# Kernel on one core of Trainium2: the first recurrence chunk is prepared before the stage barrier, the GLA normalization moves up half a unit, and the chunk state is updated behind the next chunk's inverse

## What is computed

```python
h = _rmsnorm(x, norm1_g) * (1.0 + sc1) + sh1
proj = h @ w_in                                  # IN_PROJ = 3328 + 3088 + 2048 columns
x_rwkv = p_rwkv + (prev - p_rwkv) * rwkv_mu      # token shift of the RWKV part
y_r, s_rwkv_new = _rwkv7(x_rwkv, s_rwkv, ...)    # 16 heads of 64, matrix state per head
y_g, s_gla_new = _gla(p_gla, s_gla, ...)         # 4 heads, chunks of 64
...
# _rwkv7, per row t and head:
sa = einsum('bhij,bhj->bhi', S, -kk_t)
S = S * w_t + sa * (kk_t * a_t) + v_t * k_t
y = einsum('bhij,bhj->bhi', S, r_t)
# _gla ends with
o = o * lax.rsqrt(jnp.mean(o * o, axis=-1, keepdims=True) + EPS) * norm_g
out = o.reshape(B, T, GLA_DV_TOTAL) * jax.nn.silu(r)
```

## Time and profile before

| | |
|---|---|
| median of 3 runs | 1526.92 us (1526.65, 1526.92, 1533.84) |
| the profiled execution | 1532.53 us, its span 1530.8 us |
| PE busy | 1339.8 us (88%), 13407 matmuls |
| DVE, ACT, POOL busy | 595.9, 453.4, 240.9 us |
| first block's last matmul | starts 574.37 us |
| second block's first matmul | starts 586.00 us |
| second block's first product of power 2 | starts 593.27 us |
| first expert load issued | 985.66 us |

### The profile page before, as it was taken

The page is one execution under the profiler, slowest core; times in us unless marked ns, Lnnn a source line. Parts: engine busy times, 40 slices in busy tenths (PEclk is TensorE's granted clock), DMA queues, the critical chain, the costliest instruction groups (busy, mean ns, idle before and its releaser), DMA issues. The chain is left out here.

```text
span 1530.8 us, 30353 instructions
## 1 busy us (share of the span) xinstructions
PE 1339.8 (88%) x13407; PEld 988.8 (65%) x13407; DVE 595.9 (39%) x1041; ACT 453.4 (30%) x727; POOL 240.9 (16%) x250
## 2 busy tenths in 40 slices
PE   5999999999999995888779999879888878888784
PEld 1788999898998994777769997643333323333231
DVE  3322234442235445666455658523212121221117
ACT  2333244444555453343344533200000000000002
POOL 3000000000112113334211102001111111111105
PEclk9999999999999998999899999969999988999997
DMA  8566452233422210000312391299999999999984
GB/s 322 182 202 210 131 181 83 65 109 99 143 85 70 70 36 18 4 4 4 132 30 67 104 296 52 111 405 424 427 427 425 427 426 427 426 427 427 427 369 164
DMA packets 128634, 323.05 MB, mean 211 GB/s; under 512 B 13865, under 2 KB 99075, under 8 KB 112594
## 3 DMA queue, kind: packets, MB, share of 16 engines
q1 hardware_dynamic: 114304, 289.53, 49.5%
q10 hardware_dynamic: 7522, 15.57, 2.9%
q0 software_dynamic: 6672, 15.95, 2.9%
HBM read 303.51 MB, written 25.11 MB: 215 GB/s over the span
## 5 line engine op out<-in xcount | busy, mean ns | idle before, releaser
L806 PE MATMUL bank<-upper_r 128*128 128x272 f32 x3168 | 420.0, 292 | 5.4 <-DVE upper_r L1047 5.4
L806 PEld LDWEIGHTS bank<-upper_r 128*128 128x128 f32 x3168 | 404.2, 190 | 27.7 <-issue 26.4
L2677 PE MATMUL bank<-upper7b,lower 128*64 128x512 f32 x912 | 258.2, 663 | 69.7 <-issue 68.9
L2677 PEld LDWEIGHTS bank<-upper7b,lower 128*64 128x64 f32 x912 | 83.6, 152 | 207.5 <-issue 205.3
L1024 DVE TENSOR_TENSOR upper_r<-upper,upper_r 128x1024 fp32r<-128x1024 f32 x66 | 82.1, 1244 | 284.3 <-ACT upper_r L578 284.2
L2481 ACT ACTIVATE lower<-bank 128x256 f32<-128x256 f32 x32 | 12.3, 385 | 437.6 <-PE bank L2686 437.6
L3031 DVE COPY lower<-bank 128x512 f32<-128x512 f32 x32 | 22.1, 692 | 277.6 <-PE bank L2677 277.6
L2540 PE MATMUL bank<-upper_r 128*128 128x272 f32 x768 | 102.9, 294 | 3.2 <-DVE upper_r L2926 3.2
L2540 PEld LDWEIGHTS bank<-upper_r 128*128 128x128 f32 x768 | 99.3, 191 | 5.9 <-DVE upper_r L2758 3.6
L2699 PE MATMUL bank<-upper7b,lower 128*64 128x512 f32 x432 | 98.3, 596 | 0.0
L2286 POOL DMA_INDIRECT expert_out<-lower x30 | 44.5, 1484 | 220.6 <-DVE lower L3054 210.7
(11 more groups left out here) (410 smaller groups left out, 1809.1 us busy)
## 6 DMA issues: line engine op xcount, KB each, us to landing
upper7b<-in_expert_w_gate SPq DMA_DIRECT2D x29, 2048.0 KB, 30.9
upper7b<-in_expert_w_up SPq DMA_DIRECT2D x28, 2048.0 KB, 33.1
upper7b<-in_expert_w_down SPq DMA_DIRECT2D x27, 2048.0 KB, 27.6
upper<-in_w_in SPq DMA_DIRECT2D x66, 512.0 KB, 3.8
lower<-in_w_ada SPq DMA_DIRECT2D x23, 1024.0 KB, 5.0
lower<-in_expert_w_down SPq DMA_DIRECT2D x5, 2048.0 KB, 30.0
lower<-in_expert_w_up SPq DMA_DIRECT2D x4, 2048.0 KB, 36.5
lower<-in_expert_w_gate SPq DMA_DIRECT2D x3, 2048.0 KB, 30.9
```

The costliest lines, as they stand in the source:

```text
L806: m = mm(psum[s][:, c, 0:HALF], w_part[s][:, k, :], h_part[:, k, c * HALF:(c + 1) * HALF], start=k == 0 and w_part is w_high and h_part is ...
L2677: m = nc.tensor.matmul(psum[s][64 * b:64 * b + 64, 1, :], x_t[(e // 2) % 2][:, k, s * BLK:(s + 1) * BLK], w[:, k, :], start=k == 0, stop=k ...
```

## The change

Three things are moved. (1) In the GLA the squares go from j = 7 to 6, the mean and the root from 8 to 7, the transposes and the gate product from 10 to 9; `PREP_SLOT` goes from 84 to 82, so that the preparation ends in unit 64. (2) The entry of chunk 0 (two exponentials, alphas, queries, keys, an identity) goes from behind the barrier into the first block, next to unit 65; its six semaphores outlive the barrier, and the buffers are laid out anew: the rounded operands of the projection now stand at the end of the arena, the entry's results where the weight slots and the low-rank weights were. (3) `state(c)` goes behind `inverse(c+1)` in DVE's list, with a third buffer for `lam_end`. The layout of the regions is left out of the diff.

```diff
-        PREP_SLOT = 84
+        PREP_SLOT = 82
...
-                    if 0 <= slot - GLA_SLOT - 8 * i < 11]
+                    if 0 <= slot - GLA_SLOT - 8 * i < 10]
...
+        decays = sem("decays", lasting=True)
...
+                pool.wait_ge(w_mm, KD)
+                pool.wait_ge(a_mm, KD)
+                pool.tensor_copy(ari_first[:, :, P:192], id_w.unsqueeze(1).broadcast_to([P, 8, 64])).then_inc(fixed, 1)
+                pool.wait_ge(decays, 2)
+                pool.tensor_tensor(ari_first[:, :, 64:P], p_rw[:, 0:8, 0:64], lam_c, ALU.mult).then_inc(r_done, 1)
...
-                        if j == 7:
+                        if j == 6:
                             gla_squares(i, w, nc_)
-                        if j == 8:
+                        if j == 7:
                             gla_rows(i, w, nc_)
...
+                    if u == NU - 1:
+                        act.wait_ge(bon_mm, KD)
+                        for c in range(2):
+                            nc.scalar.activation(bon[c], psum[3][32 * c:32 * c + 16, c, 0:HALF], ACT.Copy
+                                                 ).then_inc(bon_done, 1)
+                        act.wait_ge(lam_done, 2 * KD)
+                        act.wait_ge(w_split, NU)
+                        nc.scalar.activation(lam_c, lam[:, :, 0:64], ACT.Exp).then_inc(decays, 1)
+                        nc.scalar.activation(lam_i, lam[:, :, 0:64], ACT.Exp, scale=-1.0).then_inc(decays, 1)
+                        nc.scalar.activation(c_sig, c_raw, ACT.Sigmoid).then_inc(c_sig_done, 1)
                     out(u, kind, f)
...
-                        if j == 10:
+                        if j == 9:
                             pe.wait_ge(o_done, 4 * i + 4)
...
-                    if phase == 0:
+                    if phase == (0 if k else 1):
                         if k == 0:
                             v.wait_ge(mixed, 10)
                             v.wait_ge(y_g_kept, 16 * 5)
...
+                v.wait_ge(kk_done, KD)
+                v.wait_ge(w_mm, KD)
+                v.wait_ge(a_mm, KD)
+                ve.tensor_scalar(ari_first[:, :, 0:1], kk[:, :, 0:1], -1.0, None, ALU.mult).then_inc(alpha_done, 1)
+                v.wait_ge(decays, 2)
+                ve.tensor_copy(lam_end_first, lam_c[:, :, 63]).then_inc(end_done, 1)
+                ve.scalar_tensor_tensor(out=ari_first[:, :, 1:64], in0=kk[:, :, 1:64], scalar=-1.0, in1=lam_c[:, :, 0:63],
+                                        op0=ALU.mult, op1=ALU.mult).then_inc(alpha_done, 1)
+                v.wait_ge(ka_done, KD)
+                v.wait_ge(w_split, NU)
+                for n, p in enumerate((slice(0, 64), slice(64, 128))):
+                    ve.tensor_tensor(bk_first[p, :, n, :], ka[p, :, 0:64], lam_i[p], ALU.mult).then_inc(bk_done, 1)
+                    ve.tensor_tensor(bk_first[p, :, 1 - n, :], p_rw[p, 8:16, 0:64], lam_i[p], ALU.mult).then_inc(bk_done, 1)
                 v.wait_ge(ends_tr, 1)
                 ve.tensor_copy(ends_t[0:52, :], bank(4)[0:52, 0:128]).then_inc(ends_t_done, 1)
...
-                identity(0)
                 pool.memset(t64, 0.0).then_inc(fixed, 1)
...
-                queries(0)
                 identity(1)
...
-                decay(0)
                 decay(1)
...
-                    if c >= 2:
-                        v.wait_ge(s_done, c - 1)
-                    nc.vector.tensor_copy(lam_end[c % 2], lam_c[:, :, CH - 1]).then_inc(end_done, 1)
+                    if c >= 3:
+                        v.wait_ge(s_done, c - 2)
+                    nc.vector.tensor_copy(lam_end[c % 3], lam_c[:, :, CH - 1]).then_inc(end_done, 1)
...
                         power(c + 1, 2)
-                    state(c)
-                    if more:
                         masked(c + 1, 2)
...
                         inverse(c + 1)
+                    state(c)
+                    if more:
                         inverse_off(c + 1)
```

More of the change, by code:

```diff
@@ L215, in build @@
         alpha_up = sq[:, 0:512]
+        first_at = chunk_at
+        W1 = Region(first_at)
+        bk_first = W1.take(8, 2, 64)
+        lam_c = W1.take(8, 64)
+        lam_i = W1.take(8, 64)
+        W2 = Region(z_at)
+        ari_first = W2.take(8, 192)
+        lam_end_first = W2.take(8)
         xa = rkr
@@ L1201, in _ @@
                 v.wait_ge(ends_t_done, 1)
-                v.wait_ge(kk_done, KD)
         clear_semaphores()
-        lay_out_upper(3, 0, MID)
+        live.extend((decays, alpha_done, r_done, bk_done, end_done, fixed))
+        lay_out_end("3", F32)
         NCK = NCH + 1
-        S4 = Region(chunk_at)
-        ari = [S4.take(8, 192) for _ in range(3)]
-        bk = [S4.take(8, 2, CH) for _ in range(2)]
+        S4 = Region(end_at)
         z4 = [S4.take(8, 2, P) for _ in range(2)]
@@ L1220, in build @@
         u0 = S4.take(8, CH)
-        s_h = [S4.take(8, CH) for _ in range(2)]
-        s_smp = S4.take(8, CH)
-        lam_c = S4.take(8, CH)
-        lam_i = S4.take(8, CH)
-        lam_end = [S4.take(8) for _ in range(2)]
+        bk_second = S4.take(8, 2, CH)
+        S5 = Region(first_at, z_at)
+        bk = [S5.take(8, 2, CH), bk_second]
+        lam_c = S5.take(8, CH)
+        lam_i = S5.take(8, CH)
+        s_second = S5.take(8, CH)
+        s_smp = S5.take(8, CH)
+        S6 = Region(z_at, end_at)
+        ari = [S6.take(8, 192)]
+        lam_end = [S6.take(8)]
+        ari += [S6.take(8, 192) for _ in range(2)]
+        lam_end += [S6.take(8) for _ in range(2)]
+        s_h = [S6.take(8, CH), s_second]
         st_rows_in = z4[1][0:64].rearrange("i j h n -> i (j h n)")[:, 0:D].rearrange("i (j n) -> i j n", n=P)
@@ L1552, in state_rows @@
                                               psum[s][0:64, b, :]).then_inc(st_rows, 1)
-                alphas(0)
-                for p, n in zip(HEADS, range(2)):
-                    nc.vector.tensor_tensor(bk[0][p, :, n, :], ka[p, :, 0:CH], lam_i[p], ALU.mult).then_inc(bk_done, 1)
-                    nc.vector.tensor_tensor(bk[0][p, :, 1 - n, :], p_rw[p, 8:16, 0:CH], lam_i[p], ALU.mult
-                                            ).then_inc(bk_done, 1)
-                for s in range(2):
-                    v.wait_ge(spilled[s], 16 * 8)
                 first_powers(0)
@@ L1570, in _ @@
                 alphas(1)
+                for s in range(2):
+                    v.wait_ge(spilled[s], 16 * 8)
                 v.wait_ge(st_in_tr, 1)
```

49 lines of the change are left out of this document (30 added, 19 removed).

## The result

The changed kernel takes 1513.85 us (median of 4 runs, 1511.33 to 1515.15) and the kernel before, beside it, 1529.18 us; the ratio is 0.9894, 95% interval 0.9863 to 0.9925: 15.3 us less between the medians. The profiled execution took 1514.58 us, its span 1512.7.

A forecast was written before the change was run, and what follows sets the result against it. The expert-weight stream bounds the tail, so TensorE's waits before its start at 985.6 us count: GLA 10.9, entry 5.0 and chunks 1.6 sum to 17.5 us, from 1526.92 to 1509.4 us; range for 8 in 10, 1504 to 1517.

The forecast's parts named there:

- The first rival: GLA tiles 0, 3 and 4: table loads and exits make a split late, 6.0 us back, 1515.4; chance 0.11.
- the room of 0.6: GLA tile 3: the split starts at 344.2, TensorE wants unit 37's weights at 344.8, so it just fits by 0.6 us.
- The fourth: Rival: GLA waits have another releaser and chunk savings go into stalls; only 5 us won, 1521.9; chance 0.06.
- the barrier took 1.8 us, and up to 0.8 more: Barrier exit: 1.8 us behind VectorE as last engine, up to 0.8 more for SyncE's transfers; taken as 579.4.
- at 588.3: Entry: power 2 starts at 588.3 instead of 593.27, behind POOL's sum, a gain of 5.0 us.
- the second rival: Entry's gain given back at POOL's sum and by a low clock: 3.5 us back, 1512.9; chance 0.09.
- the third rival: Chunks: the state's sum blocks `by_values`, 0.3 us in each chunk, 4 us back, 1513.4; chance 0.09.
- the slower one: Rival: the moved state's operations hold TensorE at `by_values` and `by_state` in eight chunks; 1528 to some 1535; chance 0.04.
- the discount of "a third": Chunks: a third of what is saved may vanish in TensorE's stalls with no releaser, so 1.6 us taken, not 2.4.
- stalls without a releaser grow by what the waits lose: Sign that the prediction is wrong: TensorE's stalls that no engine releases grow as much as its waits shrink.
- The likeliest 1509.4: Whole kernel: all three gains, 17.5 us off a median of 1526.92; chance 0.61, own range 1504.5 to 1513.
- 22.4 us if nothing is lost in the chunks and POOL stays hidden: Whole kernel: largest gain in the likeliest case, giving the lower end of its range, 1504.5 us.

The follow-up runs named there:

- e1: Kernel before with only the GLA rows moved up half a unit, entry and chunks as before; 1517.91 us, ratio 0.9934.
- e12: Changed kernel with the four normalized copies of each GLA tile made twice; 1516.67 us, ratio 0.9896 to the kernel before.
- e6: Kernel of e5 with VectorE's copy of the last rows moved ahead of its four keys; 1501.43 us, ratio 0.9835 to the kernel before.
- e10: Changed kernel run again as it is; 1509.68 us, ratio 0.9890 to the kernel before.
- e5: Changed kernel with POOL's first sum of chunk 0 ahead of its identity copies and keys of chunk 1; 1503.67 us, ratio 0.9849 to the kernel before.
- e4: Kernel before with only the state moved behind the next chunk's inverse, and a third lam_end buffer; 1528.30 us, ratio 1.0002.
- e3: Changed kernel with the state put back between powers 2 and 3, third lam_end kept; 1513.42 us, ratio 0.9899 to the kernel before.
- e2: Changed kernel with the GLA rows at their old half units, so entry and chunk part alone; 1526.83 us, ratio 0.9998 to the kernel before.

## Why the prediction was right

**The GLA part** was predicted at 10.9 and gave 13.0 (13.0 to 14.0 in the ten profiles with the early rows and single copies; 10.3 us in e1's median). The mechanism held in each step: all waits gone, the split of tile 3 in time by 0.6 us, the loads in idle time. The term was too small because it counted waits only and not the spell at 1.2 GHz behind one of them: 10.9 and 1.7 us make 12.6 of the 13.0, and the rest is unaccounted for. The first rival, which the room of 0.6 spoke for, did not come true; e12 shows that it was near. The fourth, another releaser behind the same waits, is out with them. The drain that "ScalarE: Activation LUTs" (the Trainium skill, section What ACT_TABLE_LOAD costs) adds to each switch would have taken that room several times over: the rows show the next ACTIVATE 0.02 us behind the load, and no wait.

**The entry** was predicted at 5.0 and gave 4.2 at power 2, and 2.2 and 3.4 (two executions) at the first products with the values. Two steps were off. First, "the barrier took 1.8 us, and up to 0.8 more" for VectorE as the last engine: the exit was 2.8 us behind it, since SyncE's two transfers stand behind the very copy that had been put last (e6). TensorE's first chunk matmul so came 6.2 us behind the transpose of the ends, not 5.0. Second, power 2 "at 588.3" was meant to carry its gain on; instead TensorE ran at its lower clock for longer behind its first chunk matmul than before, and power 2, power 3 and the products between took up to 1.8 times as long, in the first execution until 21 us behind the transpose. In e10, from power 2 on, only power 3 and part of the products beside it did. That POOL's wait holds the clock down is not shown: the kernel before had one of 1.60 us at the same place and ran power 2 in 1.10. That is the second rival ("given back at POOL's sum and by a low clock"), priced at 3.5 with a chance of 0.09. It came true by 1.6 to 2.8 us. That POOL is late next was right, with 2.7 us of waits where 3 to 4 were forecast; it was worth more than that: e5 won 4 to 5 us at D.

**The chunks** were predicted at 1.6 and showed nothing that can be told from zero. The waits are as predicted to 0.01 us (0.35 a chunk), `by_values` waits for nothing, so the third rival and the slower one are out (e4: 1.0002). The step that failed is the discount of "a third" for stalls: stalls and clock together scatter by more than the term. The prediction had named a sign of being wrong, "stalls without a releaser grow by what the waits lose", and in the chunks it came: from 18.2 us before to 21.6 and 19.7 in the two executions, while the waits by cause fell from 11.3 to 8.7 and 9.2. It is scatter as much as an exchange, for with the state back and the waits at 11.0 (e3) the stalls were 20.8.

**The sum** of 17.5 was nearly right partly by luck, by errors that cancel: GLA 2 too small, entry 2 to 3 and chunks 1.6 too large. The likeliest 1509.4 stood on a median of before of 1526.92 from three runs, while 25 runs give 1528.26; beside e10's 1509.68 it was 1527.31. The "22.4 us if nothing is lost in the chunks and POOL stays hidden" does not follow from the terms, which give 10.9 + 6.6 + 2.4 = 19.9.

## What to carry to other kernels

A short wait of TensorE costs its length and, where the clock falls behind it, most of that again (here 1.7 us on 2.4); so waits removed from a busy stretch can give more than their sum. Waits close behind a barrier, for an engine that is late there, gave back part of what the barrier won. When work is moved ahead of a barrier, look at what stands first in each queue behind it, and at what the last engine to arrive releases in turn (here a DMA): two reorderings there (e5, e6) were worth about half as much as the whole change. And a term of 2 us in a stage whose two executions differ by 3.6 can't be read from one pair of traces; count waits by cause, and let repeated runs decide on the time.

## What was unexpected of the hardware

- The lower clock comes in spells, not only after long gaps: 2.4 us without work in an otherwise full stretch was followed by one that cost 1.7 us. Nor does a gap's length alone decide it: 2.8 us in the same stretch was followed by none, and in e2, with the same waits, four spells came where the kernel before had one.
- After a barrier's 5.9 us gap the granted clock stayed at 0.50 of full for 16 us (566.5 to 582.5) while TensorE had waits of 0.9 and 1.9 us. In another execution of the same kernel (e10), with the same waits, it was back before power 2 and fell again behind it; in e5, without them, it was back before power 2, less than five microseconds behind the first matmul, and fell again ten microseconds later.
- A burst of 4.9 MB of loads, which holds the DMA engines for 0.86 of 17 us, goes with a stall of TensorE of about 4 us, in which nothing in the program is late.
